# Two mixer stages of a recurrent trunk: whole-tile turns, paired memory products, and two elementwise jobs moved to other engines

## What is computed

```python
# RWKV-7 group, 8 heads of 64: a delta-rule recurrence over tokens
sa = einsum('bhvk,bhk->bhv', S, -kk_t)
S  = S * w_t + sa * (kk_t * a_t) + v_t * k_t           # y_t = S r_t
# mLSTM group, 4 heads of 128, chunked
num = g_inter * (q @ C) + (q k^T * gates) @ v
h   = num / max(|den|, exp(-m));  h = (h - mean(h)) * rsqrt(var(h) + eps)
C   = dec * C + sum_s ws_s k_s v_s^T                    # memory, per head 128 x 128
```

## Time and profile before

| quantity | value |
|---|---|
| runs of the kernel | 1550.63 us median of 3 (1549.57 to 1556.33) |
| span of the profiled execution | 1551.5 us |
| PE busy | 1489.7 us, 96% of the span |
| DVE busy | 982.2 us, 63% |
| ACT busy | 696.5 us, 45% |
| POOL busy | 375.1 us, 24% |
| mean granted TensorE clock | 0.975 of full |
| mixer stage of the first layer | about 379 to 500 us of the span |
| mixer stage of the second layer | about 1138 to 1265 us |

### The profile page before, as it was taken

One profiled execution on the slowest core, in us unless ns is written; L12 is line 12 of the kernel. 1 busy time (PEld: TensorE's weight loads), 2 busy tenths in 40 slices (PEclk: granted clock), 3 DMA queues, 4 the chain that ended last, 5 costly groups with the idle time before them and its releaser, 6 DMA issues.

```text
span 1551.5 us, 34978 instructions
## 1 busy us (share of the span) xinstructions
PE 1489.7 (96%) x13874; PEld 1434.4 (92%) x13874; DVE 982.2 (63%) x1571; ACT 696.5 (45%) x1198; POOL 375.1 (24%) x395
## 2 busy tenths in 40 slices
PE   7999998999889999999999999989988999999995
PEld 7999998999778999999999999989988789999995
DVE  4444445587276787776577775466944667877644
ACT  4333334755545543334343334367563355333332
POOL 4222472011241422221322221200142304222100
PEclk9999999999998999999999999999999799999998
DMA  8555542553123655444545545534430434545451
GB/s 216 149 149 149 165 149 69 136 137 96 32 60 91 167 157 154 137 148 136 169 138 147 149 149 164 149 96 109 109 85 3 120 86 143 170 138 164 144 163 34
DMA packets 318846, 198.89 MB, mean 128 GB/s; under 512 B 7696, under 2 KB 303664, under 8 KB 318736
## 3 DMA queue, kind: packets, MB, share of 16 engines
q1 hardware_dynamic: 315120, 190.69, 42.2%
q0 software_dynamic: 3616, 6.62, 2.0%
HBM read 188.50 MB, written 8.78 MB: 127 GB/s over the span
## 4 chain that ended last, share of the span: by engine, by line
PE 83%; DVE 8%; ACT 5%; DVEq 2%; issue 2%; DMA 0%; ACTq 0%; SPq 0%
PE bank L2047 23%; PE bank L2049 23%; PE bank L2048 23%; DVE wlo L2538 2%; PE bank L2134 1%; PE bank L630 1%; PE bank L725 1%; ACT whi L2337 1%; DVE rlo L2569 1%; PE bank L2139 1%; PE bank L455 1%; ACT z L1133 1%; PE bank L740 1%; PE bank L755 1%; PE bank L737 1%
## 5 line engine op out<-in xcount | busy, mean ns | idle before, releaser
L2337 ACT ACTIVATE whi<-raw 128x1024 fp32r<-128x1024 f32 x340 | 358.8, 1060 | 470.3 <-PE bank L2049 453.9
L2538 DVE TENSOR_TENSOR wlo<-raw,whi 128x1024 fp32r<-128x1024 f32 x340 | 421.7, 1244 | 228.5 <-ACT whi L2337 227.7
L2047 PE MATMUL bank<-rhi,whi 128*128 128x322 f32 x984 | 306.5, 311 | 0.0
L2049 PE MATMUL bank<-rhi,wlo 128*128 128x322 f32 x984 | 305.9, 311 | 0.0
L2048 PE MATMUL bank<-rlo,whi 128*128 128x322 f32 x984 | 304.8, 310 | 0.0
L2047 PE MATMUL bank<-xh,whi 128*128 128x320 f32 x912 | 285.3, 313 | 5.8 <-DVE xl L2712 3.5
L2048 PE MATMUL bank<-xl,whi 128*128 128x320 f32 x912 | 282.2, 309 | 0.0
L2049 PE MATMUL bank<-xh,wlo 128*128 128x320 f32 x912 | 282.2, 309 | 0.0
L2807 POOL TENSOR_TENSOR hl<-scratch,hh 128x320 f32 x88 | 146.8, 1668 | 496.4 <-DVE scratch L2659 379.7
L2047 PE MATMUL bank<-hh,whi 128*128 128x320 f32 (+1 forms) x704 | 218.4, 310 | 0.5 <-DVE wlo L2538 0.5
L2048 PE MATMUL bank<-hl,whi 128*128 128x320 f32 (+1 forms) x704 | 217.4, 309 | 0.0
(11 more groups left out here) (411 smaller groups left out, 1960.3 us busy)
## 6 DMA issues: line engine op xcount, KB each, us to landing
raw<-in_ffn_wg SPq DMA_DIRECT2D x88, 512.0 KB, 3.8
raw<-in_ffn_wu SPq DMA_DIRECT2D x88, 512.0 KB, 3.8
raw<-in_ffn_wd SPq DMA_DIRECT2D x88, 512.0 KB, 3.7
raw<-in_w_in SPq DMA_DIRECT2D x60, 512.0 KB, 3.8
raw<-in_w_out SPq DMA_DIRECT2D x16, 512.0 KB, 6.4
raw<-in_state_C SPq DMA_DIRECT2D x8, 512.0 KB, 6.2
out_s_C<-raw SPq DMA_DIRECT2D x8, 512.0 KB, 3.8
ring<-in_state_wkv POOLq DMA_DIRECT2D x2, 1024.0 KB, 8.3
```

The costliest lines, as they stand in the source:

```text
L2047: pe.matmul(out, w_hi, hi, start=start, stop=False)
L2049: return pe.matmul(out, w_lo, hi, start=False, stop=stop)
L2337: act.activation(whi[:, slot, :], raw[:, slot, :], ACT.Copy).then_inc(hi_ready.sem, 1)
L2538: dve.tensor_tensor(wlo[:, slot, :], raw[:, slot, :], whi[:, slot, :].bitcast(F32), ALU.subtract).then_inc(lo_ready.sem, 1)
```

## The change

It has six parts, all in the mixer stages.

1. The keys' turns become whole-tile turns: POOL writes `bkh` with the two key kinds swapped for the upper 64 partitions (8 instructions in place of 3), so that one 128 x 128 transpose for each head pair does what four 64 x 64 blocks did. Ten key sides become five.
2. The samples' RWKV memories are loaded with four transfers in place of one, in an order in which a 128 x 128 transpose turns two head pairs; 16 matrix instructions of a memory side become 4 transposes.
3. The sides are 19, not 24, and stand at other steps (`SIDE_AT`): keys at 9, 10, 11, 13, 14, the products `RV` at 15 to 17, tails at 19, memories at 20, 21, 23, 24.
4. Two heads' sample keys and values lie on the lower and the upper 64 partitions (two more turns each for keys and values, small extra copies on ACT, one more gate column for each pair). The eight products `C` are then issued as four pairs, the two of a pair on different partition halves and in different banks. `masked_values` makes two heads at once on 128 partitions, so there are two instead of four.
5. POOL decays the memories ahead of the products: eight `decayed_memory` multiplications (128 x 512, in place), after `samples_of_heads`. DVE then adds each product with one `tensor_tensor` of 128 x 512 instead of four `scalar_tensor_tensor`.
6. ACT squares the mLSTM heads (`head_squares`, after its copy of steps 17 and 24) in place of DVE's L1492.

The diff, cut to these parts:

```diff
-        vmask = [area(1536, SB, DK, rows=TS, of=spare), area(15304, SB, DK, rows=TS)]
+        vmask = [area(1536, SB, DK, of=spare), area(15304, SB, DK)]
...
             for h in range(HB):
                 last = turn(pe, bank[4 + n][0:rows, h * DK:(h + 1) * DK], qk[:, HB + h, at:at + rows])
+                if n == 2 and h % 2 == 0:
+                    last = turn(pe, bank[4 + n][PART[1], h * DK:(h + 1) * DK], qk[:, HB + h + 1, at:at + rows])
...
+                if n == 2 and h % 2 == 0:
+                    last = pe.matmul(bank[5][PART[1], h * DK:(h + 1) * DK], mv[:, h + 1, at:at + rows], ident[:, :],
+                                     start=True, stop=True)
...
             if kind == "C":
-                pe.wait_ge(vmask_ready.sem, vmask_ready.by(L, i // 2 + 1))
-                last = pe.matmul(b[:, :], kt[0:TS, 2, i // 2, :], vmask[(i // 2) % 2][:, 4 * (i % 2):4 * (i % 2) + 4, :],
+                g, half, q = i // 4, i // 2 % 2, i % 2
+                pe.wait_ge(vmask_ready.sem, vmask_ready.by(L, g + 1))
+                last = pe.matmul(b[:, :], kt[PART[q], 2, 2 * g, :], vmask[g][PART[q], 4 * half:4 * half + 4, :],
                                  start=True, stop=True)
...
-        VALUES, KEYS, RVS, ENDS, MEMS = 1, 1 + NCH, 1 + 3 * NCH, 4 + 3 * NCH, 5 + 3 * NCH
+        VALUES, KEYS, RVS, ENDS, MEMS = 1, 1 + NCH, 1 + 2 * NCH, 4 + 2 * NCH, 5 + 2 * NCH
         NSIDE = MEMS + SB // 2
-        SIDE_AT = [*range(KEYS), *range(KEYS + 3, NSIDE + 3)]
+        SIDE_AT = [*range(KEYS), 9, 10, 11, 13, 14, 15, 16, 17, 19, 20, 21, 23, 24]
...
-                c, q = (k - KEYS) // 2, (k - KEYS) % 2
                 for j in range(NJ):
-                    for kind in range(2):
-                        last = pe.matmul(b[PART[q ^ kind], j * NA:(j + 1) * NA], bkh[PART[q], j, c, kind, :],
-                                         ident[PART[q], PART[q]], start=True, stop=True)
+                    last = pe.transpose(b[:, j * P:(j + 1) * P],
+                                        bkh[:, j, k - KEYS, :, :].rearrange("p s t -> p (s t)"), ident[:, :])
...
-                    for j in range(NJ):
-                        for part in PART:
-                            at = (i * NJ + j) * NA
-                            last = pe.matmul(b[part, at:at + NA], wkv_rows[part, 2 * (k - MEMS) + i, j, :],
-                                             ident[part, part], start=True, stop=True)
+                    for jj in range(NJ // 2):
+                        at = (i * NJ // 2 + jj) * P
+                        last = pe.transpose(b[:, at:at + P], wkv_rows[:, 2 * (k - MEMS) + i, jj, :], ident[:, :])
...
+            if n == 2:
+                for h in range(0, HB, 2):
+                    last = act.activation(kt[PART[1], 2, h, :], bank[6][PART[1], h * DK:(h + 1) * DK], ACT.Identity,
+                                          scale=cols[PART[1], 2, 2, h:h + 1])
...
+            if n == 2:
+                act.activation(va[PART[1], 2, 0:HB:2, 0:DK],
+                               bank[5][PART[1], :].rearrange("p (h d) -> p h d", h=HB)[:, 0:HB:2, :], ACT.Copy)
...
+        def head_squares(act, L, g):
+
+            rows, tiles, n, stat, heads, wide = head_views(g)
+            act.wait_ge(hmean_ready.sem, hmean_ready.by(L, g + 1))
+            if g == 0:
+                act.wait_ge(side_copied.sem, side_copied.by(L, RVS))
+            act.activation(hsq[0:rows, 0:n * DK].rearrange("p (h d) -> p h d", d=DK), heads[:, :, 0:DK],
+                           ACT.Square).then_inc(hsq_ready.sem, 1)
...
+        SQUARES_AT = (17, 24)
         ROOTS_AT = (19, 25)
...
-            if g == 0:
-                dve.wait_ge(side_copied.sem, side_copied.by(L, RVS))
-            tt(squares_, heads[:, :, 0:DK], heads[:, :, 0:DK], ALU.mult)
-            dve.drain()
+            dve.wait_ge(hsq_ready.sem, hsq_ready.by(L, g + 1))
             dve.tensor_reduce(stat(2), squares_, AX_X, ALU.add)
...
-                for k in range(4):
-                    s = 4 * half + k
-                    at = h * TS + s * ST + ST - 1
-                    last = dve.scalar_tensor_tensor(out=C0[:, h, s, :], in0=C0[:, h, s, :], scalar=rexp[:, at:at + 1],
-                                                    in1=b[:, k * DK:(k + 1) * DK], op0=ALU.mult, op1=ALU.add)
+                own = C0[:, h, 4 * half:4 * half + 4, :].rearrange("p b e -> p (b e)")
+                dve.wait_ge(memory_decayed.sem, memory_decayed.by(L, i + 1))
+                last = dve.tensor_tensor(own, own, b[:, :], ALU.add)
...
-        def masked_values(pool, L, h):
+        def masked_values(pool, L, g):
-            values = va[0:TS, 2, h, 0:DK].rearrange("t (o e) -> t o e", o=1)
-            own = bmask[0:TS, :].rearrange("t (b o) -> t b o", o=1)
-            pool.tensor_tensor(vmask[h % 2], bcast(values, 1, SB), bcast(own, 2, DK),
+            values = va[:, 2, 2 * g, 0:DK].rearrange("t (o e) -> t o e", o=1)
+            own = bmask[:, :].rearrange("t (b o) -> t b o", o=1)
+            pool.tensor_tensor(vmask[g], bcast(values, 1, SB), bcast(own, 2, DK),
                                ALU.mult).then_inc(vmask_ready.sem, 1)
+        def decayed_memory(pool, L, i):
+
+            h, half = 2 * (i // 4) + i % 2, i // 2 % 2
+            own = C0[:, h, 4 * half:4 * half + 4, :]
+            at = h * TS + 4 * half * ST
+            decay_ = rexp[:, at:at + 4 * ST].rearrange("p (b t) -> p b t", t=ST)[:, :, ST - 1:ST]
+            pool.tensor_tensor(own, own, bcast(decay_, 2, DK), ALU.mult).then_inc(memory_decayed.sem, 1)
...
-            pool.tensor_tensor(two(bkh[:, :, 0:NPC, :, :]), two(bk[:, :, 0:NPC, :, :]),
-                               bcast(dlast[:, :, 0:NPC].rearrange("p j (c o) -> p j c o", o=1), 3, 2 * CH), ALU.mult)
             for s in range(2):
+                pool.tensor_tensor(bkh[PART[0], :, 0:NPC, s, :], bk[PART[0], :, 0:NPC, s, :],
+                                   bcast(dlast[PART[0], :, 0:NPC].rearrange("p j (c o) -> p j c o", o=1), 3, CH),
+                                   ALU.mult)
+                pool.tensor_tensor(bkh[PART[1], :, 0:NPC, s, :], bk[PART[1], :, 0:NPC, 1 - s, :],
+                                   bcast(dlast[PART[1], :, 0:NPC].rearrange("p j (c o) -> p j c o", o=1), 3, CH),
+                                   ALU.mult)
...
-            dma(wkv_rows[:, :, :, :].rearrange("p b j k -> p (b j) k"),
-                lay(I["state_wkv"]).rearrange("l b (j q) v k -> (q v) (l b j) k", q=2)).then_inc(wkv_in.sem, 16)
+            for a, part in enumerate(PART):
+                for q in range(2):
+                    src = lay(I["state_wkv"]).rearrange("l b (j h) v k -> v (l b j) h k", h=4)
+                    dma(wkv_rows[part, :, :, q * NA:(q + 1) * NA].rearrange("p b j k -> p (b j) k"),
+                        src[:, :, 2 * a + q, :]).then_inc(wkv_in.sem, 16)
...
             pool.wait_ge(side_copied.sem, side_copied.by(L, RVS))
             masked_values(pool, L, 0)
             pool.wait_ge(num_mm.sem, num_mm.by(L, NTT))
+            decayed_memory(pool, L, 0)
+            decayed_memory(pool, L, 1)
             masked_values(pool, L, 1)
-            pool.wait_ge(left_mm.sem, left_mm.by(L, 2))
-            masked_values(pool, L, 2)
-            pool.wait_ge(left_mm.sem, left_mm.by(L, 4))
-            masked_values(pool, L, 3)
+            for i in range(2, 2 * HB):
+                decayed_memory(pool, L, i)
             pool.drain()
...
-                    sp.wait_ge(left_done.sem, left_done.by(L, LEFT.index(("C", 2 * h + 1)) + 1))
+                    sp.wait_ge(left_done.sem, left_done.by(L, LEFT.index(("C", 4 * (h // 2) + 2 + h % 2)) + 1))
```

More of the change, by code:

```diff
@@ L359, in hymba_kernel @@
         inter_read = signal("inter_read", 1)
+        hmean_ready = signal("hmean_ready", 2)
+        hsq_ready = signal("hsq_ready", 2)
         hvar_ready = signal("hvar_ready", 2)
@@ L524, in gate_columns @@
                     last = turn(pe, bank[4][0:rows, (n * 3 + q) * HB:(n * 3 + q + 1) * HB], row[:, q, at:at + rows])
+            for h in range(0, HB, 2):
+                own = 8 * HB + h
+                last = pe.matmul(bank[4][PART[1], own:own + 1], row[:, 2, 2 * P:T], sel[:, h + 1, 0:1],
+                                 start=True, stop=True)
             last.then_inc(cols_turned.sem, 1)
@@ L1040, in copy_gate_columns @@
                 last = act.activation(cols[0:rows, n, 1:3, :], src[:, 1:3, :], ACT.Exp)
+            last = act.activation(cols[PART[1], 2, 2, 0:HB:2], bank[4][PART[1], 8 * HB:9 * HB:2], ACT.Exp)
             last.then_inc(cols_ready.sem, 1)
@@ L1110, in copy_side @@
             elif k < RVS:
-                c, q = (k - KEYS) // 2, (k - KEYS) % 2
-                last = act.activation(bkt[c][:, :, q, :], heads4(b), ACT.Copy)
+                last = act.activation(bkt[k - KEYS][:, :, :, :].rearrange("p j q n -> p (j q n)"), b[:, :], ACT.Copy)
             elif k < ENDS:
@@ L1863, in pool_mixers @@
```

(11 more changed lines are left out.)

20 lines of the change are left out of this document (12 added, 8 removed).

## The result

The changed kernel takes 1557.70 us, median of 19 runs (1552.20 to 1560.89), against 1551.12 us for the kernel before, also of 19 (1549.32 to 1557.50). The ratio is 1.0028, 95% interval 1.0017 to 1.0039: slower by less than half a percent, but above the range of the forecast. The profiled execution took 1557.53 us; its span is 1555.8 us (1551.5 before), its mean granted clock 0.968 (0.975).

The account below looks back on a forecast made before the run. It took DVE's squares and additions and PE's `C` products as the bounding chain, with POOL's port contention. Terms of -1.1 us a layer and -2.5 for pairs in layer two gave -4.7: 1546 us, range 1536 to 1556.

Parts of the forecast that it names:

- POOL's decays: Around step 19, POOL's train holds DVE's small L1496 and L1498: +1.5 us a layer, plus +0.5 at step 20.
- its second rival: POOL's port becomes the bound, PE's gap at step 19 passes 3.0 us, both layers lose clock: 1559 us, chance 0.10.
- own signs of being wrong: DVE's small instructions at 0.15 us, clock 0.50 in layer one's steps 20-24 or 1.00 in layer two's, start not later.
- Second head group: Squares leave DVE, -0.7 us; a POOL memory term may hold the means, +1.0 us (0 to 2.0), a layer.
- The clock: Layer terms taken at full clock; half clock counted only in the second layer, where pairs gain 2.5 us.
- Start of the stage: Added key and value turns on PE and copies on ACT: +1.0 us a layer, bounds 0 and 1.5.
- The early masked product: POOL's first masked product holds L1423, +1.0, while step 18 loses a side, -0.5: net +0.5 us, bounds 0 and 1.0.
- Squares: First group's squares move from DVE to ACT: -1.4 us a layer, bounds -1.5 and -1.1.
- L1508 and L1510: At step 20 these DVE instructions may wait for POOL's train: +0.5 us a layer, bounds 0 to 2.0.
- Additions: DVE's memory additions get shorter, four pairs at 0.87 us: -3.5 us a layer, half if PE's products end those steps.
- Pairs: Paired `C` products on PE: 0.9 us each, hidden at full clock; 2.5 us gained in the half-clock second layer.
- Sides at 0: Shorter, fewer key and memory sides on PE lie beside DVE's work in steps 20 to 24: 0, uncovered -1.8 us.

Follow-up runs that it names:

- Version 1: Changed kernel with two waits added on POOL, so its decays and second masked product run after the first head group's variance or scaled heads: 1549.39 us.
- version 4: Changed kernel with POOL's decays, masked products and memory terms moved later, plus DVE's first-group sum of squares taken four times: 1556.44 us.
- version 2: Changed kernel with two of POOL's memory terms made to wait for the second head group's centred and scaled heads: 1553.76 us.
- version 8: Changed kernel with POOL's decays, masked products and memory terms reordered, then the decays fused with the additions on DVE again: 1549.20 us.
- 13: Kernel before with POOL's masked products and memory terms later, plus whole-tile turns alone in the change's order of sides: 1556.58 us.
- 6: Kernel before with only POOL's order changed: first two masked products and second and third memory terms made to wait: 1543.70 us.
- 14: Kernel before with POOL's work later, whole-tile turns and ACT's squares, the sides laid over steps 18 and 19 again: 1543.43 us.
- 11: Kernel before with POOL's work later, plus whole-tile turns with the change's order of sides and ACT's squares: 1551.72 us.
- 15: Changed kernel with POOL's decays, masked products and memory terms later, plus later sides, including steps 18 and 19: 1547.37 us.
- 3: Changed kernel with POOL's decays, both masked products and two memory terms moved behind DVE's instructions: 1542.85 us.
- version 5: Changed kernel without second heads on the upper partitions: one head at a time in `C`, four masked products on POOL: 1574.09 us.
- version 7: Changed kernel with POOL's work moved later and single heads in `C`, third and fourth masked products behind all decays: 1551.49 us.

## Why the prediction was wrong

Between the forecast of -4.7 us and the +4.3 of the profiled spans lie 9.0 us. By the first table 3.5 of them are in the first layer's steps 17 to 26, 2.5 in its steps 0 to 17, 2.5 behind step 26 of the two layers, and the rest elsewhere.

**POOL's decays: here it failed.** The prediction let L1496 and L1498 each "wait for the rest of one instruction: 0 to 1.9 + 1.0 us together" and took +1.5. Three instructions waited, not two: the third, `tensor_scalar` with one operand in SBUF, was left out of the term. Against 0.41, 0.17 and 0.17 us before, 1.90, 0.93 and 0.93 make +3.01, over the upper bound. That is the case of its second rival, the port as the bound with PE's pause beyond 3.0 us in both layers, priced at 1559 and given 0.10. One of the prediction's own signs of being wrong came with it, a clock of 0.50 behind the pause in the first layer. Version 1 shows the cause (the products moved, the three instructions at 0.17, -8 us) and version 4 that such a pause is enough for the fall of the clock behind it, with no POOL product beside DVE.

**Second head group.** +1.0, bounds 0 and 2.0. By the rows L1508, L1511 and L1534 took 0.88, 0.70 and 0.90 us more than free of POOL (version 2): +2.5, again over the upper bound. Version 2 gained 3.9 us for both layers together, with the clock.

**The clock.** The sum kept the first layer's clock and gave the end of the inversion no term; there the clock was down for 24 and 17 us, where it had been 14 and 7. Version 2 takes away the pause of step 25 and 7 us of the first layer's fall, no more; that pause is not its whole cause, and the rest stays open. The table's last column, an estimate, puts the changed kernel 1.2 us under the kernel before at equal clock, and 5.6 us of the loss to its lower clock. By that estimate the forecast failed less in its engine work than in what the pauses do to PE.

The smaller terms:

- **Start of the stage:** +1.0 forecast, +1.34 and +1.35 measured, inside its bounds.
- **The early masked product:** L1452 took 1.32 us instead of 0.42, held by POOL's masked product (435.73 to 437.63), as forecast. The rest of the +3.0 in the first layer's steps 0 to 17 goes with the clock, down for 6.8 us around 414 in place of 3.4. The pauses ahead of that place are the same in both layers (1.63 and 1.28 us, then 1.25 and 1.29 in the kernel before), and in the second layer the fall was missing and the stretch unchanged in spite of the hold; what makes it stays open.
- **Squares:** ACT's took 1.06 us, the price of the earlier trace rows; DVE waits 0.61 where it worked 2.57, -2.0 for -1.4, better than its bound.
- **L1508 and L1510** (now L1534 and L1536): 0.49 and 1.98 for 0.17 and 1.23, +1.1, inside its bounds.
- **Additions:** 1.27 for two halves, as forecast, but PE's products ended half of those steps (version 8), a case that the prediction named and didn't take.
- **Pairs:** 1.11 us at full clock and 2.08 at half, as forecast. That the second layer's steps 17 to 26 came to -5.5 for -5.1 is luck in part: DVE's holds were larger than in the sum, and the clock was down for 10 us there, not 17. (The signs that the prediction names, 29 and 34 us for these steps, don't follow from its own terms, which give 28.1 and 32.6.)

**Sides at 0.** The prediction asked only whether they lie on the chain. Beside that they gave PE work in steps 18 and 19, and with single products, taking them from there costs (13 against 6, which also changes the turns themselves) and putting them back gains (14 against 11). In the changed kernel with POOL quiet the order doesn't help (15 against 3).

## What to carry to other kernels

Before work goes to POOL, list every DVE instruction that comes due beside it, the tiny ones with a single SBUF operand too, and let POOL start behind them: two added waits gave 8 us here, and reordering POOL in the old kernel alone gave as much as the six changes and the reordering together. A pause of PE costs its length and then the clock, so price both; and a part that takes work from PE during a pause may cost time. Undo parts one by one only in a version without holds: single heads in the changed kernel (1574 us) measured POOL, not the heads.

## What the runs showed of the hardware

- A DVE instruction of 128 x 8 beside a train of POOL products can be passed over by several of them: 6.93 us in version 5 (six products), 1.90 in the changed kernel (one), 0.17 with POOL idle. `tensor_tensor`, `scalar_tensor_tensor` and `tensor_scalar` from SBUF were held; `tensor_reduce` (1.22 us at 443.49, inside two decays) and `reciprocal` (0.17 at 466.38, inside a memory term) were not. The Trainium skill, SBUF — State Buffer, section "SBUF: two separate sides", says that the shared ports go to one of the two engines for a whole instruction, and counts DVE's two-port modes beside two SBUF inputs; the 0.93 us of L1526, one product of POOL, agree if it runs in such a mode, which no run here shows; the 6.93 us are more than one instruction.
- Pauses of 4.47 us or more had a granted clock of 0.50 in them or right behind them in all eight layers that had them (the changed kernel, versions 2, 4 and 5). After about 1.2 us at step 19 it fell in some layers and not in others with the same instructions (version 7: not after 1.21 us in the first layer, but after 1.22 us in the second). How long it stayed down differed: 3.4 us with pairs (versions 3 and 8), 7 to 14 with single products (versions 7 and 11); that the products make the difference is not shown.
- The runs of one kernel spread over 4 to 13 us, and their mean clocks with them (0.001 for 1.01 us).
